# Norm products split so that they run during the squares, FFN products kept in PSUM, one array for the bias tables, one squares operation for block 0

## The reference, cut to what matters

```python
for l in range(2):                       # first kind
    z = rms_norm(x, norm1_g[l]) @ w_in[l]
    # latent attention, gated linear attention, state-space branch, gated merge
    x = x + merged @ w_out[l]
    h2 = rms_norm(x, norm2_g[l])
    x = x + square(relu(h2 @ w_ff1[l])) @ w_ff2[l]          # 4096 hidden
# second kind: GLU + convolution, dilated attention with a relative bias table, gated merge
x = x + rms_norm(merged @ w_mix_out, g_post_mix)
h = rms_norm(x, g_pre_ffn)
gate, up = split(h @ w_ffn_in)                              # 2816 hidden each
x = x + rms_norm((silu(gate) * up) @ w_ffn_out, g_post_ffn)
```

## Time and profile before

| what | us |
|---|---|
| median of 3 runs (1539.19 to 1540.39) | 1540.09 |
| the profiled execution, its own time | 1536.8 |
| its span | 1535.0 |
| PE busy in the span | 1485.0 (97%) |
| DVE, ACT, POOL busy | 889.6, 698.4, 882.8 |

### The profile page before, as it was taken

The page is one execution under the profiler, slowest core; times in us unless marked ns, Lnnn a source line. Parts: engine busy times, 40 slices in busy tenths (PEclk is TensorE's granted clock), DMA queues, the critical chain, the costliest instruction groups (busy, mean ns, idle before and its releaser), DMA issues.

```text
span 1535.0 us, 23998 instructions
## 1 busy us (share of the span) xinstructions
PE 1485.0 (97%) x9775; PEld 1317.3 (86%) x9775; DVE 889.6 (58%) x1407; ACT 698.4 (45%) x1052; POOL 882.8 (58%) x364
## 2 busy tenths in 40 slices
PE   7999999999999999999999999999999999899997
PEld 6977778889899897777788888989999988799996
DVE  5878875443433687886434455338993454265545
ACT  6544222554444654422255344464445655554443
...
DMA packets 321784, 234.47 MB, mean 153 GB/s; under 512 B 9676, under 2 KB 305131, under 8 KB 321674
## 3 DMA queue, kind: packets, MB, share of 16 engines
...
...
## 4 chain that ended last, share of the span: by engine, by line
PE 84%; issue 5%; ACT 4%; POOL 4%; DVE 2%; DMA 1%; SPq 0%; POOLq 0%; DVEq 0%; ACTq 0%
PE ps L672 18%; PE ps L1943 14%; PE ps L1059 7%; PE ps L1060 7%; PE ps L1061 7%; PE ps L1926 6%; PE ps L1928 6%; PE ps L1927 6%; POOL w_lo L1283 4%; PE ps L1134 1%; PE ps L1171 1%; PE ps L2063 1%; PE ps L2077 1%; ACT w_hi L1317 1%; PE ps L2044 1%
## 5 line engine op out<-in xcount | busy, mean ns | idle before, releaser
L1283 POOL TENSOR_TENSOR w_lo<-raw,w_hi 128x1024 fp32r<-128x1024 f32 (+1 forms) x206 | 504.6, 2467 | 499.6 <-ACT w_hi L1317 497.2
L751 POOL TENSOR_TENSOR w_lo<-raw,w_hi 128x1024 fp32r<-128x1024 f32 x154 | 378.0, 2468 | 138.3 <-ACT w_hi L773 132.8
L1317 ACT ACTIVATE w_hi<-raw 128x1024 fp32r<-128x1024 f32 (+1 forms) x206 | 218.1, 1060 | 241.6 <-PE ps L672 75.8
L1059 PE MATMUL ps<-h_hi,w_hi 128*128 128x256 f32 x864 | 246.3, 285 | 1.8 <-DVE h_lo L928 1.3
L1060 PE MATMUL ps<-h_lo,w_hi 128*128 128x256 f32 x864 | 244.3, 283 | 0.0
L1061 PE MATMUL ps<-h_hi,w_lo 128*128 128x256 f32 x864 | 244.2, 283 | 0.0
L1926 PE MATMUL ps<-h_hi,w_hi 128*128 128x256 f32 (+1 forms) x816 | 233.3, 286 | 6.4 <-POOL w_lo L1283 4.3
L1927 PE MATMUL ps<-h_lo,w_hi 128*128 128x256 f32 (+1 forms) x816 | 231.3, 283 | 0.0
L1928 PE MATMUL ps<-h_hi,w_lo 128*128 128x256 f32 (+1 forms) x816 | 231.2, 283 | 0.0
L773 ACT ACTIVATE w_hi<-raw 128x1024 fp32r<-128x1024 f32 x154 | 162.0, 1059 | 116.2 <-PE ps L1061 43.3
L1943 PE MATMUL ps<-hN,raw 128*128 128x256 f32 x768 | 174.9, 383 | 0.0
...
## 6 DMA issues: line engine op xcount, KB each, us to landing
raw<-in_w_in_dram SPq DMA_DIRECT2D x160, 512.0 KB, 3.8
raw<-in_w_ff_dram SPq DMA_DIRECT2D x128, 512.0 KB, 4.1
...
```

The source lines that it names most:

```text
L751: nc.gpsimd.tensor_tensor(out=w_lo[(NS * L + i) % RING][:, 0:kt * n], in0=raw[(NS * L + i) % RING][:, 0:kt * n], in1=w_hi[(NS * L + i) % R ...
L1059: MM(out, w[0], x[0], start=first_k, stop=False, skip_group_check=skip)
L1283: nc.gpsimd.tensor_tensor(out=w_lo[(NS * l + i) % RING][:, 0:kt * n], in0=raw[(NS * l + i) % RING][:, 0:kt * n], in1=w_hi[(NS * l + i) % R ...
L1317: A_(w_hi[(NS * l + i) % RING][:, 0:kt * n], raw[(NS * l + i) % RING][:, 0:kt * n], ACT.Copy)\
```

## The change

It has seven parts.

1. `norm_rows` of block 0: one square over 1024 columns, which waits for both quarters of x, in place of two of 512, and no Identity.
2. `post_norm` on ACT: squares of 512 columns, the first of a block with an Identity behind it. On DVE: `y * g` for both quarters as soon as their squares are done; behind the row factor, `y * rs + x` in one operation per quarter.
3. FFN of the second kind: ACT writes only the tanh; DVE reads gate and up from PSUM, and its product lies in the up pair. PE waits for DVE's `ff2_ok` where it waited for ACT's copy.
4. FFN of the first kind: DVE writes relu times the product into the pair of PSUM, and rounds from there. PE waits for `ff_sq`.
5. The bias tables come as one array of 99 x 408 that the host has filled; six small DMAs and the three of `second_bias` are gone.
6. The load of ACT's table for Ln and Exp stands behind unit 4's squares and no longer behind unit 1.
7. DVE's product for the latents stands between the two parts of k = 7.

```diff
@@ -594,15 +594,21 @@
             n = 2 * (2 * k + b)
             c = [nt[:, 2 * n + i:2 * n + i + 1] for i in range(4)]
...
+            if b == 0:
+                act.wait_ge(*ready(1))
+                A_(sqt[:, 0, :], xt[:, 0, :], ACT.Square, accum_out=c[2]).then_inc(norm_sq.s, 2)
+                act.wait_ge(norm_sq.s, norm_sq(l, n + 2))
+                A_(c[3], c[2], ACT.Ln, scale=1.0 / DM, bias=C("eps")).then_inc(norm_ln.s, 2)
+            else:
+                act.wait_ge(*ready(2 * b))
+                A_(tok(sqt, 2 * b), tok(xt, 2 * b), ACT.Square, accum_out=c[0]).then_inc(norm_sq.s, 1)
...
@@ -694,19 +700,8 @@
         def second_tables(sp):
-            sp.dma_start(oneh, oneh_dram[:, 0:384]).then_inc(tab_in.s, 16)
-            for g in range(3):
-                sp.dma_start(tabl[33 * g:33 * g + 32, :], oneh_dram[33 * g:33 * g + 32, 384:408]).then_inc(tab_z.s, 16)
-            for g in range(3):
-                sp.dma_start(tabl[33 * g + 32:33 * g + 33, :], oneh_dram[33 * g + 32:33 * g + 33, 384:408])\
-                    .then_inc(tab_in.s, 16)
+            sp.dma_start(PT2[0][0:99, 0:408], A["bias_tables"]).then_inc(tab_in.s, 16)
...
-            for g in range(3):
-                sp.dma_start(tabl[33 * g:33 * g + 32, 8 * g:8 * g + 8],
-                             A["rel_bias_table_2"][:, 8 * g:8 * g + 8]).then_inc(tab_in.s, 16)
@@ -802,15 +797,22 @@
             def post_norm(k, slab):
                 act.preload_act_table_set("natural_log_exp_and_others")
                 for b in range(NT):
-                    if b == 0:
-                        act.wait_ge(tm_out.s, tm_out(L, 3 * k - 1))
-                    else:
-                        act.wait_ge(used.s, used(L, slab + 1))
-                    c = slice(16 + b, 17 + b)
-                    link(A_(sqt[:, b, :], ps_half(k, b), ACT.Square, accum_out=nt[:, c]))
-                    link(A_(nt[:, c], nt[:, c], ACT.Ln, scale=1.0 / DM, bias=C("eps4" if k == 1 else "eps")))
-                    A_(nt[:, c], nt[:, c], ACT.Exp, scale=-0.5).then_inc(post_rs.s, 1)
+                    rs_, part = nt[:, 16 + b:17 + b], nt[:, 18 + b:19 + b]
+                    for i in (2 * b, 2 * b + 1):
+                        if i < 3:
+                            act.wait_ge(tm_out.s, tm_out(L, 3 * (k - 1) + i + 1))
+                        else:
+                            act.wait_ge(used.s, used(L, slab + 1))
+                        y = ps_out(i) if k == 1 else ps_tok(i)
+                        A_(tok(sqt, i), y, ACT.Square, accum_out=rs_ if i % 2 else part).then_inc(post_sq.s, 1)
+                        if i % 2 == 0:
+                            act.wait_ge(post_sq.s, n + i + 1)
+                            link(A_(part, part, ACT.Identity, scale=1.0 / DM, bias=C("eps4" if k == 1 else "eps")))
+                    act.wait_ge(post_sq.s, n + 2 * b + 2)
+                    link(A_(rs_, rs_, ACT.Ln, scale=1.0 / DM, bias=part))
+                    A_(rs_, rs_, ACT.Exp, scale=-0.5).then_inc(post_rs.s, 1)
@@ -905,10 +907,9 @@
                 if c >= 2:
                     act.wait_ge(ff2_ok.s, c - 1)
                 u = V_FF + 2 * c
-                th, gt, up_ = ffb[c % 2]
-                evacuate(u, up2_at(c) + 1, [(gt, pair(u % 3), ACT.Copy, {}),
-                                            (th, pair(u % 3), ACT.Tanh, dict(scale=0.5))])
-                evacuate(u + 1, up2_at(c) + 3, [(up_, pair((u + 1) % 3), ACT.Copy, {})])
+                th = ffb[c % 2][0]
+                evacuate(u, up2_at(c) + 1, [(th, pair(u % 3), ACT.Tanh, dict(scale=0.5))])
+                prep(up2_at(c) + 3 + RING)
@@ -929,15 +930,17 @@
             def post_norm(k):
-                for i in range(4):
-                    b = i // 2
-                    if i % 2 == 0:
-                        dve.wait_ge(post_rs.s, 2 * (k - 1) + b + 1)
-                    y = ps_out(i) if k == 1 else ps_tok(i)
-                    stt(y, y, nt[:, 16 + b:17 + b], gp[:, k - 1, 512 * (i % 2):512 * (i % 2) + 512],
-                        ALU.mult, ALU.mult).then_inc(post_pr.s, 1)
-                    dve.wait_ge(post_pr.s, 4 * (k - 1) + i + 1)
-                    tt(tok(xt, i), tok(xt, i), y, ALU.add).then_inc(post_ok.s, 1)
+                n = 4 * (k - 1)
+                for b in range(NT):
+                    for i in (2 * b, 2 * b + 1):
+                        y = ps_out(i) if k == 1 else ps_tok(i)
+                        dve.wait_ge(post_sq.s, n + i + 1)
+                        tt(y, y, gp[:, k - 1, 512 * (i % 2):512 * (i % 2) + 512], ALU.mult).then_inc(post_pr.s, 1)
+                    dve.wait_ge(post_rs.s, 2 * (k - 1) + b + 1)
+                    for i in (2 * b, 2 * b + 1):
+                        y = ps_out(i) if k == 1 else ps_tok(i)
+                        dve.wait_ge(post_pr.s, n + i + 1)
+                        stt(tok(xt, i), y, nt[:, 16 + b:17 + b], tok(xt, i), ALU.mult, ALU.add).then_inc(post_ok.s, 1)
             for c in range(NC2):
-                th, gt, up_ = ffb[c % 2]
-                dve.wait_ge(evac.s, evac(L, V_FF + 2 * c + 2))
+                th, gt, _ = ffb[c % 2]
+                gate, up_ = pair((V_FF + 2 * c) % 3), pair((V_FF + 2 * c + 1) % 3)
+                dve.wait_ge(evac.s, evac(L, V_FF + c + 1))
                 if c >= 2:
                     dve.wait_ge(used.s, used(L, down2_at(c - 2) + 2))
-                link(stt(gt, th, 1.0, gt, ALU.add, ALU.mult))
-                link(tt(gt, gt, up_, ALU.mult))
-                link(V.tensor_scalar(f_hi[c % 2][:, :, :], gt, 0.5, None, ALU.mult))
-                stt(f_lo[c % 2][:, :, :], gt, 0.5, f_hi[c % 2][:, :, :], ALU.mult, ALU.subtract).then_inc(ff2_ok.s, 1)
+                link(stt(gt, th, 1.0, gate, ALU.add, ALU.mult))
+                dve.wait_ge(used.s, used(L, up2_at(c) + 4))
+                link(tt(up_, gt, up_, ALU.mult))
+                link(V.tensor_scalar(f_hi[c % 2][:, :, :], up_, 0.5, None, ALU.mult))
+                stt(f_lo[c % 2][:, :, :], up_, 0.5, f_hi[c % 2][:, :, :], ALU.mult, ALU.subtract).then_inc(ff2_ok.s, 1)
@@ -1186,7 +1191,10 @@
             def up(c):
                 for s in range(2):
                     u = V_FF + 2 * c + s
-                    free(u)
+                    if u - V_FF < 3:
+                        free(u)
+                    else:
+                        pe.wait_ge(ff2_ok.s, c - 1 + s)
                     if i == I_FF + 12 and l == DEPTH - 1:
                         second_tables(sp)
-                    if i == I_FF + 17 and l == DEPTH - 1:
-                        sp.wait_ge(tab_z.s, 48)
-                        second_bias(sp)
@@ -1375,6 +1380,7 @@
                         link(A_(SP(P_PC), SP(P_TA), ACT.Sin, scale=-1.0, bias=C("halfpi")), l)
                         A_(SP(P_SQ), SP(P_PC), ACT.Square)
                         A_(SS(S_SQ), SS(S_PS), ACT.Square).then_inc(lam_s.s, 1)
+                    if u == 4:
                         act.preload_act_table_set("natural_log_exp_and_others")
                 for k in range(8):
-                    if k == 7:
-
-                        dve.wait_ge(lat_rs.s, lat_rs(l, 1))
-                        for j in range(5):
...
-                        ins.then_inc(of_ok.s, 1)
                     n = 1 << k
                     parts = 1 if k < 7 else 2
                     for part in range(parts):
+                        if part:
+                            dve.wait_ge(lat_rs.s, lat_rs(l, 1))
...
+                            ins.then_inc(of_ok.s, 1)
                 for c in range(NCH):
-                    f = fr[:, c % 2, :, :]
+                    x = pair((U_FF + c) % PGF)
                     dve.wait_ge(evac.s, evac(l, U_FF + c + 1))
                     if c >= 2:
                         dve.wait_ge(used.s, used(l, down_at(c - 2) + 2))
-                    link(tt(f, f, f, ALU.mult))
-                    link(V.tensor_copy(f_hi[c % 2][:, :, :], f))
-                    split_lo(f_lo[c % 2][:, :, :], f, f_hi[c % 2][:, :, :]).then_inc(ff_sq.s, 1)
+                    link(tt(x, fr[:, c % 2, :, :], x, ALU.mult))
+                    link(V.tensor_copy(f_hi[c % 2][:, :, :], x))
+                    split_lo(f_lo[c % 2][:, :, :], x, f_hi[c % 2][:, :, :]).then_inc(ff_sq.s, 1)
@@ -2294,15 +2299,17 @@
                     for m in range(2):
                         i = up_at(c) + m
                         weights(l, i)
-                        if m == 0:
+                        if m == 0 and c < 2:
                             free(l, U_FF + c)
+                        elif m == 0:
+                            pe.wait_ge(ff_sq.s, ff_sq(l, c - 1))
-                        pe.wait_ge(tab_in.s, 16 * 8)
+                        pe.wait_ge(tab_in.s, 16 * 2)
+    tables = distance_table()
+    for g in range(3):
+        tables[33 * g:33 * g + 32, 384 + 8 * g:392 + 8 * g] = _np.asarray(inputs["rel_bias_table_2"])[:, 8 * g:8 * g + 8]
+    laid_out["bias_tables"] = tables
```

35 lines of the change are left out of this document (16 added, 19 removed).

## The result

The changed kernel took 1527.87 us (median of 4 runs, 1527.37 to 1531.1), the kernel before 1540.24 in 4 runs beside it: ratio 0.9926, 95% interval 0.9908 to 0.9943.

What follows compares the result with a forecast made beforehand. PE bounds the kernel, busy 1485.0 of 1535.0 us, so only its waits can be won. 2.56 + 2.3 + 1.3 + 0.5 + 0.5 - 0.75 = 6.4 us, from 1540.09 to 1533.7; range 1531 to 1535.5 (8 in 10: 1530.3 to 1536.3).

Steps and rivals of the forecast that it cites:

- behind the stalls of 2.13 and 2.30 us PE went on at full speed: Z stage's unit 2 and last chunk: PE's clock stays up behind these waits, so no clock gain was counted there.
- The change is the same in it: The gain of 6.4 us applies equally to the median of 1540.09, 3.3 above the profiled execution, giving 1533.7.
- Table load: Z stage of both layers: moving ACT's load behind unit 4 shortens PE's wait behind unit 2, 2 x 1.28 = 2.56 us.
- rival 2: Z stage: PE's slack at unit 4 is too small, so 2 x 1.28 is given back, 1536.3; chance 0.09.
- Last chunk: Second FFN's last chunk: PE's wait for DVE goes, as operations with an operand in PSUM are shorter, 2.3 us.
- Rival 3: Second FFN: DVE takes 2.88 per operation, so PE waits at chunk 1 and the last chunk, 1539.7; chance 0.04.
- End: Last norm: only two DVE operations stand behind the row factor, 1.3 us won, bounds 0.7 and 1.5.
- Tables: Layer 1's FFN: fewer SP issues let a late load land earlier, 0.5 us with the clock, bounds 0 and 3.7.
- Rivals 1 and 4: Layer 1's FFN: SP's issues set the landing, 1530.5, chance 0.15; or one engine serves the new table, 1542.3, chance 0.03.
- POOL: FFNs of the first kind: POOL freed of DVE's two-operand work, felt in layer 1, 0.5 us, bounds 0 and 1.3.
- Block 0's squares: Norms of block 0: one square makes Ln 0.15 us later at five norms, 0.75 us lost, bounds 0 and 1.5.

Runs made afterwards that it cites:

- experiment 1: The kernel before, unchanged, run once more beside itself: 1537.20 us against 1537.21, ratio 1.0001.
- experiment 4: The kernel before with only the bias tables loaded as one array: 1537.12 us, ratio 0.9989 to the kernel before.
- experiment 7: The kernel before with only the second FFN's part (gate and up read from PSUM, PE waits for `ff2_ok`): 1533.58 us, ratio 0.9969.
- experiment 9: The kernel before with only the norm behind projections changed (`post_norm`): 1535.00 us against 1537.54, ratio 0.9984.
- experiment 8: The changed kernel with the convolution weights loaded in two parts, 16 and 15 rows: 1526.60 us, ratio 0.9925 to the kernel before.

## Why the prediction was wrong

It forecast 6.4 us; the repeated comparisons give 9.0 and 8.5 by the medians, the first 12.4. Two errors, of different kinds.

**The clock.** The step of the prediction that failed is the sentence "behind the stalls of 2.13 and 2.30 us PE went on at full speed". It was read off layer 1 and carried over to layer 0, where the trace had the opposite: the window 36.60:40.20 above, and in the earlier trace rows the matmul at 36.68, which takes 0.48 us where the one at 532.95 takes 0.39. Over the profiled executions with these waits unfilled, the clock fell behind unit 2 in 5 of 7 in layer 0 and in 4 of 7 in layer 1, behind the last chunk's 2.30 us in 4 of 7, behind layer 1's 2.3 to 3.3 us in 6 of 9, and behind the changed kernel's 1.9 to 2.1 there in 1 of 3. A fall costs about 1.45 us in the z stage and in the second FFN. The change takes away three of the four places and shortens the fourth: (5/7 + 4/7 + 4/7) + (6/9 - 1/3) = 2.2 falls fewer on the mean, times 1.45 is 3.2 us. That is an estimate from few executions, above all the 1 in 3. The mean clocks say about the same: 0.9939 over 88 executions of the kernel before, 0.9965 over 13 of the changed one, and a fall of 3.4 us to half is 1.7 / 1536 = 1.1 thousandths, so 2.6 of them would be 2.4 falls. About 0.5 of the 2.6 lie in the tail, where PE is done: in the profiles the clock is at half in the last 3.0 to 4.6 us where the end is as before, and in the last 2.2 of the changed kernel. That leaves 1.9 falls. The prediction had 0.2 for this, in the term of the tables. The fault was to let one profile, in which the clock stayed up behind two such waits of four, stand for all executions: experiment 1 has it up behind three of them, experiment 4 down behind three.

**The reference point.** "The change is the same in it" was said of the median 1540.09. Three executions gave it then, and a fourth lay beside them (1539.2 to 1540.4), but of 88 later ones only 17 were at 1539.2 or more, and their median is 1537.5. Against that the changed kernel's 1527.87 is 9.7 less. Why those four came so high is not settled: more falls of the clock would do it (longer executions have the lower clock), or something of that chip. The first comparison gave no clocks for them.

**Term by term**, without the clock:

- Table load, 2.56: right in mechanism, measured 2.8 (2 x 1.41; each wait fell by 1.40, the load's 1.28 and what stood around it). Unit 4 had the slack, and rival 2 did not come.
- Last chunk, 2.3: measured 3.1. A wait in brackets is counted from the modelled end of the matmul before, 0.40 us after its start, while the next could have started 0.23 after it, and the two matmuls behind it took 0.74 and not 0.63; so 2.30 of wait was 2.56 of time. The other 0.56 was a wait near 1347 for `w_lo`, which the prediction does not have: ahead of the copy to `w_hi`, ACT had copied the gate at 1342.49 and only then loaded the table for Tanh, 1.28 us at 1343.09, so POOL began at 1346.01. Without the copy of the gate the load runs while ACT waits for PE, and POOL begins 1.9 us earlier, counted from the stage's first product (7.8 us behind it in experiment 7, 9.7 before). Rival 3 did not come: all operations took 0.69 us.
- End, 1.3: measured 1.2, and 1.5 where it is the only change (experiment 9).
- Tables, 0.5: 0.1 or less. The reason, one engine for 31 rows, was right in substance and experiment 8 bears it out. In the changed kernel the load lands 0.5 us earlier and the wait is 1.9 to 2.1, as forecast, but the stretch's length is hardly less (193.69 against 193.8): what the wait gives up comes back in a later wait for `w_lo` (1.41 us at 927; 0.98 at 931 in experiment 7). In the changed kernel with the old table load the wait is 2.47 and in the kernel before with the new tables 2.49, so it is not the tables alone that shorten it. Rivals 1 and 4 are out.
- POOL, 0.5: 0.2 in layer 0, nothing that shows in layer 1.
- Block 0's squares, 0.75 lost: 0.28 at layer 1's start, and 0.2 and 0.5 by the stretches ahead of the two FFNs, where POOL's waits scatter by as much. Behind the mix it was said to be near the same: in fact the split of `post_norm` costs 0.6 there (experiment 9), and the single square takes 0.45 of it back.

The sum is best taken over the stretches, at full clock: 2.8 (z stages) + 3.1 (second FFN) + 1.2 (end) + 0.1 (layer 1's FFN), less 0.2, 0.1 and 0.5 (the three stretches with a norm of block 0 ahead of an FFN or of layer 1's z stage, two squares against one, means over all profiled kernels) and 0.2 (behind the mix) = 6.2. With the 3.2 of the clock it is 9.4. The means over all timed executions are 1537.84 (88) and 1528.47 (13), 9.4 apart; that the two agree to a tenth is luck, as the clock's term is known to half a microsecond at best. So is part of the closeness of 6.4 and 6.2: the last chunk gave 0.8 more than forecast, tables and POOL together about as much less. The 6.4 was about right for the waits and left out what stands behind them.
